# Norm statistics with tokens on the partitions, and two weight jobs run side by side behind six norms

## The reference, cut to what matters

```python
D_MODEL = 1024; SEQ = 512; CTX_LEN = 256; LN_EPS = 1e-5; EPS = 1e-6

def _layer_norm(x, g, b):
    mu = jnp.mean(xf, axis=-1, keepdims=True)
    var = jnp.mean(jnp.square(xf - mu), axis=-1, keepdims=True)
    return (xf - mu) * lax.rsqrt(var + LN_EPS) * g + b

def _rms(x, g):
    return xf * lax.rsqrt(jnp.mean(xf * xf, axis=-1, keepdims=True) + EPS) * g

# layers 0 and 1 (first_block), layer i
u = x * (1.0 + sc1) + sh1
y = mixer(u)                      # 0: mLSTM, 1: differential attention
x = _layer_norm(ALPHA * x + (1.0 + g1) * y, ...)
u = x * (1.0 + sc2) + sh2
y = _conv_ffn(u, ...)             # up-projection 1024 -> 5632, conv, gelu gate, down
x = _layer_norm(ALPHA * x + (1.0 + g2) * y, ...)

# layers 2 and 3 (second_block), for x and, but at the end, for ctx
hx = _rms(x, g) * (1 + cx1) + sx1
x = x + gx1 * mixer(hx)           # 2: conv + Fourier, 3: neighbourhood attention
x = x + gx2 * _mlp(_rms(x, g) * (1 + cx2) + sx2, w1, w2)
```

## Time and profile before

| | |
|---|---|
| median of 3 runs | 3028.05 us (3025.34 to 3028.12) |
| the profiled execution: its time / its span | 3022.47 us / 3020.7 us |
| PE (matmul) busy | 2818.6 us, 93% of the span |
| VectorE, ScalarE, GpSimd busy | 1595.3, 1088.2, 1072.0 us |
| granted TensorE clock, mean | 0.971 of full |
| chain of waits that ended last | PE 84%, VectorE 8%, ScalarE 4% |

### The profile page before, as it was taken

How to read it: one execution, slowest core, us unless ns; L and a number is a source line. 1 busy time by engine, 2 the same in 40 slices (tenths; PEclk the granted TensorE clock), 3 DMA queues, 4 the chain that set the end, 5 groups by cost and what they waited for, 6 DMA issues and landing times.

```text
span 3020.7 us, 38114 instructions
## 1 busy us (share of the span) xinstructions
PE 2818.6 (93%) x13754; PEld 2269.5 (75%) x13754; DVE 1595.3 (53%) x2262; ACT 1088.2 (36%) x1738; POOL 1072.0 (35%) x462
## 2 busy tenths in 40 slices
PE   4998899998998899998899799999997999989998
PEld 3885588886776578886686688888885877768887
DVE  6537796855455797975422422754453376431111
ACT  3333443333465543333411422222224337543222
POOL 2440444444521544444221132323232223334443
PEclk9999999998999899999899899999997999999999
DMA  5350355532421255532111122333331122122222
GB/s 212 113 188 28 118 202 194 191 126 86 142 84 43 98 181 195 188 118 91 44 63 59 39 84 77 127 124 125 123 128 49 63 68 91 54 76 97 98 97 84
DMA packets 89947, 329.70 MB, mean 109 GB/s; under 512 B 9956, under 2 KB 10724, under 8 KB 89320
## 3 DMA queue, kind: packets, MB, share of 16 engines
q1 hardware_dynamic: 85392, 312.21, 30.0%
q10 hardware_dynamic: 4440, 16.00, 1.7%
HBM read 324.50 MB, written 2.10 MB: 108 GB/s over the span
## 4 chain that ended last, share of the span: by engine, by line
PE 84%; DVE 8%; ACT 4%; issue 2%; DMA 1%; POOL 1%; DVEq 0%; ACTq 0%; SPq 0%; POOLq 0%
PE bank L1363 58%; PE junk L1365 9%; PE bank L1104 2%; PE bank L1089 2%; PE bank L1254 1%; PE bank L1380 1%; PE bank L1208 1%; PE junk L1270 1%; PE bank L1287 1%; PE bank L1228 1%; ACT UF L848 1%; PE bank L1130 1%; ACT Uh L848 1%; DVE ADA L1454 1%; DMA ADA<-in_ast 1%
## 5 line engine op out<-in xcount | busy, mean ns | idle before, releaser
L491 POOL TENSOR_TENSOR WL<-RAW,WH 128x1024 fp32r<-128x1024 f32 x392 | 984.1, 2511 | 1740.3 <-ACT WH L792 1249.2
L792 ACT ACTIVATE WH<-RAW 128x1024 fp32r<-128x1024 f32 x292 | 307.0, 1051 | 384.2 <-PE junk L1365 192.0
L1363 PE MATMUL bank<-U1h,WH 128*128 128x512 f32 x960 | 377.7, 393 | 18.7 <-DVE U1l L1736 18.5
L1363 PE MATMUL bank<-U1l,WH 128*128 128x512 f32 x960 | 375.2, 391 | 0.0
L1363 PE MATMUL bank<-U1h,WL 128*128 128x512 f32 x960 | 375.1, 391 | 0.0
L1363 PE MATMUL bank<-Uh,WH 128*128 128x512 f32 x768 | 315.8, 411 | 55.2 <-DVE Ul L1738 54.7
L1363 PE MATMUL bank<-Hh,WH 128*128 128x512 f32 x864 | 342.2, 396 | 11.7 <-DVE Hl L577 11.7
L1363 PE MATMUL bank<-Hl,WH 128*128 128x512 f32 x864 | 339.6, 393 | 0.0
L1363 PE MATMUL bank<-Hh,WL 128*128 128x512 f32 x864 | 338.6, 392 | 0.0
L1363 PE MATMUL bank<-Ul,WH 128*128 128x512 f32 x768 | 307.2, 400 | 0.0
L1363 PE MATMUL bank<-Uh,WL 128*128 128x512 f32 x768 | 306.3, 399 | 0.0
(11 more groups left out here) (348 smaller groups left out, 5002.4 us busy)
## 6 DMA issues: line engine op xcount, KB each, us to landing
RAW<-in_wst SPq DMA_DIRECT2D x392, 512.0 KB, 3.4
ADA<-in_ast SPq DMA_DIRECT2D x192, 512.0 KB, 4.5
NB<-in_nbias ACTq DMA_DIRECT2D x8, 768.0 KB, 4.3
XT<-in_xt SPq DMA_DIRECT2D x1, 2048.0 KB, 15.3
STRIP<-in_strip ACTq DMA_DIRECT2D x8, 256.0 KB, 2.7
CB<-in_cb ACTq DMA_DIRECT2D x4, 512.0 KB, 4.1
DX<-in_dx ACTq DMA_DIRECT2D x1, 2048.0 KB, 7.7
out_xt<-XT SPq DMA_DIRECT2D x1, 2048.0 KB, 6.2
```

Source lines behind the costliest of these rows:

```text
L491: pool.tensor_tensor(WL[:, s4], RAW[:, s2], WH[:, s4].bitcast(F32), ALU.subtract)\
L792: act.activation(WH[:, c % 4], RAW[:, c % 2], ACT.Copy).then_inc(S("hi_done"), 1)
L1363: mm = pe.matmul(bank_of(p, u)[:], w[:, u, k], x[:, k, 0:T], start=st and m == 0, stop=en and m == 2)
```

## The change

Three things.

1. The sums of squares are turned round. `token_sums` uses a block of 128 tokens of the squares as the stationary operand and one column of MEAN as the moving one, so that the result has 128 tokens on the partitions and one column a block: 4 columns for x, 2 more for the context. Root and reciprocal then work on 128x4 or 128x6 elements (SM) in place of 128x512 or 128x768. `widen` brings the result back to one column a token on all partitions: the stationary operand is the scale column read 128 times, the moving one the identity. It lies in PSUM (bank 2 for a LayerNorm, banks 4 and 7 for an RMS norm), where the products now read it. The tile RS is gone. The mean's matmul stays.
2. In a LayerNorm VectorE adds the squares of tiles 5, 6 and 7 onto tile 4 (three instructions behind the centring), so that TensorE sums five tiles and not eight. LayerNorm 3's own sums now come ahead of the context's.
3. Behind six norms (all but LayerNorm 1, whose next phase has its own order) `side_by_side` runs the first two jobs together: for each input tile both jobs' matmuls, once the weights of both are there. Jobs 2 and 3 of the round follow as before. The first round of these phases is peeled out of its loop.

```diff
-                act.activation(RS[:, 0:T], BANK[6][:], ACT.Sqrt, bias=prm("eps5")).then_inc(S("std_done"), 1)
+                act.activation(SM[:, 48:52], BANK[6][:, 0:4], ACT.Sqrt, bias=prm("eps5")).then_inc(S("token_root"), 1)
...
-                steps.link(act.activation(RS[:, 0:T], BANK[5][:], ACT.Sqrt, bias=prm("eps6")))
...
+                n = 6 if ctx else 4
+                act.activation(SM[:, 48:48 + n], BANK[5][:, 0:n], ACT.Sqrt, bias=prm("eps6")).then_inc(S("token_root"), 1)
...
+            def side_by_side(p):
+
+                xh, xl = (U1h, U1l) if p["layer"] < 2 else (Uh, Ul)
+                for u in range(2):
+                    pe.wait_ge(S("lo_done"), p["j0"] + u + 1)
+                pe.wait_ge(S("bank_read"), p["j0"])
+                for k in range(KT):
+                    pe.wait_ge(S("u_ready"), p["fill"] + k + 1)
+                    for u in range(2):
+                        for m, (w, x) in enumerate(((WH, xh), (WH, xl), (WL, xh))):
+                            st, en = k == 0 and m == 0, k == KT - 1 and m == 2
+                            mm = pe.matmul(bank_of(p, u)[:], w[:, u, k], x[:, k, 0:T], start=st, stop=en)
+                            if p["ctx"]:
+                                mm = pe.matmul(BANK[2 + u][:, 0:C], w[:, u, k], x[:, k, T:TC], start=st, stop=en)
+                        if k == KT - 1:
+                            mm.then_inc(S("pe_job"), 1)
...
+            def token_sums(bank, c0, squares, start, stop):
+
+                n = squares.shape[-1] // P
+                for b in range(n):
+                    mm = pe.matmul(bank[:, c0 + b:c0 + b + 1], squares[:, b * P:(b + 1) * P], MEAN[:, 0:1],
+                                   start=start and b == 0, stop=stop and b == n - 1)
+                return mm
+
+            def widen(n, bank, cbank):
+
+                pe.wait_ge(S("token_scale"), n)
+                for b in range(6 if cbank is not None else 4):
+                    dst = (bank if b < 4 else cbank)[:, b % 4 * P:(b % 4 + 1) * P]
+                    ident, scale = bass.broadcast_tensor_aps(IDENT[:], SM[:, 56 + b:57 + b])
+                    mm = pe.matmul(dst, scale, ident, start=True, stop=True)
+                mm.then_inc(S("scale_wide"), 1)
...
                 pe.matmul(BANK[5][:], MEAN[:], ZS[:, 0:T], start=True, stop=True).then_inc(S("mean_sum"), 1)
+                for t in range(5):
+                    if t < 4:
+                        pe.wait_ge(S("squared"), 8 * idx + t + 1)
+                    else:
+                        pe.wait_ge(S("square_rest"), idx + 1)
+                    mm = token_sums(BANK[6], 0, SQ[:, t], t == 0, t == 4)
+                mm.then_inc(S("var_sum"), 1)
                 if idx == 3:
                     for t in range(KT):
                         pe.wait_ge(S("ctx_sq"), t + 1)
-                        pe.matmul(BANK[3][:, 0:C], MEAN[:], UF[:, t, T:TC], start=t == 0, stop=t == KT - 1)
-                for t in range(KT):
-                    pe.wait_ge(S("squared"), 8 * idx + t + 1)
-                    mm = pe.matmul(BANK[6][:], MEAN[:], SQ[:, t], start=t == 0, stop=t == KT - 1)
-                mm.then_inc(S("var_sum"), 1)
+                        token_sums(BANK[5], 4, UF[:, t, T:TC], t == 0, t == KT - 1)
+                widen(idx + 1, BANK[2], None)
...
-                mm = pe.matmul(BANK[5][:], MEAN[:], ZS[:, 0:T], start=True, stop=True)
-                if ctx:
-                    mm = pe.matmul(BANK[6][:, 0:C], MEAN[:], ZS[:, T:TC], start=True, stop=True)
+                mm = token_sums(BANK[5], 0, ZS[:, 0:TC if ctx else T], True, True)
                 mm.then_inc(S("ms_sum"), 1)
+                widen(5 + k, BANK[4], BANK[7] if ctx else None)
...
-                            mm = pe.matmul(BANK[5][:], MEAN[:], UF[:, t, 0:T], start=t == 0, stop=t == KT - 1)
+                            mm = token_sums(BANK[5], 0, UF[:, t, 0:T], t == 0, t == KT - 1)
                         mm.then_inc(S("ms_sum"), 1)
+                        widen(5, BANK[4], BANK[7])
...
-                dve.wait_ge(S("std_done"), idx + 1)
-                link(dve.reciprocal(RS[:, 0:T], RS[:, 0:T]))
+                for t in range(5, KT):
+                    dve.wait_ge(S("squared"), 8 * idx + t + 1)
+                    link(dve.tensor_tensor(SQ[:, 4], SQ[:, 4], SQ[:, t], ALU.add))
+                dve.sem_inc(S("square_rest"), 1)
+                token_scale(idx + 1, 4)
                 for t in range(KT):
-                    dve.tensor_tensor(XT[:, t], XT[:, t], RS[:, 0:T], ALU.mult).then_inc(S("normed"), 1)
+                    dve.tensor_tensor(XT[:, t], XT[:, t], BANK[2][:], ALU.mult).then_inc(S("normed"), 1)
...
+            def token_scale(n, w):
+
+                dve.wait_ge(S("token_root"), n)
+                dve.reciprocal(SM[:, 56:56 + w], SM[:, 48:48 + w]).then_inc(S("token_scale"), 1)
+                dve.wait_ge(S("scale_wide"), n)
```

More of the change, by code:

```diff
@@ L238, in build @@
         TT = at("TT", [2, TC], A_T)
-        RS = at("RS", [TC], A_T)
         UF = at("UF", [KT, TC], A_Y)
@@ L375, in first, with starts_behind_norm @@
             return p["kind"] == kind and p["layer"] == layer and not (p.get("group") or 0)
+        def starts_behind_norm(p):
+            return any(first(p, *what) for what in (("up", 0), ("up", 1), ("ab", 2), ("mlp_up", 2), ("na_q", 3), ("mlp_up", 3)))
         NA_J_END = next((p["j0"] for p in PHASES if first(p, "res2", 3)))
@@ L840, in rms_act @@
                 act.wait_ge(S("ms_sum"), k + 1)
-                steps.link(act.activation(RS[:, 0:T], BANK[5][:], ACT.Sqrt, bias=prm("eps6")))
-                if ctx:
-                    steps.link(act.activation(RS[:, T:TC], BANK[6 if k else 3][:, 0:C], ACT.Sqrt, bias=prm("eps6")))
-                act.sem_inc(S("rms_root"), 1)
+                n = 6 if ctx else 4
+                act.activation(SM[:, 48:48 + n], BANK[5][:, 0:n], ACT.Sqrt, bias=prm("eps6")).then_inc(S("token_root"), 1)
                 for t in range(KT):
@@ L1347, in head_norm_pe @@
                 mm.then_inc(S("n_ms"), 1)
+            def side_by_side(p):
[13 more added lines that the diff above has]
+                            mm.then_inc(S("pe_job"), 1)
             def stream(i, p):
-                for u in range(4):
+                after_norm = is_first(i) and starts_behind_norm(p)
+                if after_norm:
+                    side_by_side(p)
+                for u in range(2 if after_norm else 0, 4):
                     j = i * 4 + (p["j0"] + u)
@@ L1417, in _ @@
                 else:
-                    rounds(pe, p["n"] // 4, lambda i, p=p: stream(i, p), peel=peeled(p) or p["kind"] in ("v", "na_k"))
+                    rounds(pe, p["n"] // 4, lambda i, p=p: stream(i, p), peel=peeled(p) or p["kind"] in ("v", "na_k") or starts_behind_norm(p))
                 if p["kind"] == "v":
@@ L1745, in rms @@
                 w = TC if ctx else T
-                dve.wait_ge(S("rms_root"), k + 1)
-                link(dve.reciprocal(RS[:, 0:w], RS[:, 0:w]))
+                token_scale(5 + k, 6 if ctx else 4)
                 for t in range(KT):
@@ L1754, in rms @@
                                                 XT[:, t].rearrange("p (r w) -> p r w", r=ROWS),
-                                                RS[:, 0:T].rearrange("p (r w) -> p r w", r=ROWS), ALU.mult)
+                                                BANK[4][:].rearrange("p (r w) -> p r w", r=ROWS), ALU.mult)
                     else:
-                        ins = dve.tensor_tensor(UF[:, t, 0:T], XT[:, t], RS[:, 0:T], ALU.mult)
+                        ins = dve.tensor_tensor(UF[:, t, 0:T], XT[:, t], BANK[4][:], ALU.mult)
                     if ctx:
-                        ins = dve.tensor_tensor(UF[:, t, T:TC], CT[:, t], RS[:, T:TC], ALU.mult)
+                        ins = dve.tensor_tensor(UF[:, t, T:TC], CT[:, t], BANK[7][:, 0:C], ALU.mult)
                     ins.then_inc(S("rms_normed"), 1)
```

## The result

The changed kernel takes 2983.2 us (median of 4 runs) against 3026.7 for the kernel before on the same chip: a ratio of 0.986 [0.983, 0.989], 43.5 us less, where 31 were forecast. Measured once more later (after_again), again beside the kernel before, it took 2989.9 against 3016.6: 26.7 us less. The median of all eight runs after is 2988.4, that of all 35 runs before 3025.3: 37 us. The profiled execution after took 2977.8 us, its span 2976.0.

What follows compares the result with a forecast made beforehand. TensorE's work (84% of the chain of waits) plus holes at eight norms bound the kernel. Statistics 7.1 and side-by-side jobs 24.2 make 31.3 us off 3028.05: 2997 us; forecast 2983 to 3011, range with rivals A and B 2963 to 3017.

Steps and rivals of the forecast that it cites:

- Unit price and clock: New sums and widen: a small fp32 load-and-matmul pair costs 0.11 us at full clock, 0.21 us at half.
- Rival A: Faster side, for the new sums: full clock or 0.11 us a pair, 2967 us; chance 0.2.
- rival C: Slower side: load and matmul of a pair don't overlap, 0.54 us a pair at half clock, 3117 us; chance 0.07.
- Root to product: LayerNorms: root, reciprocal, handovers and widen up to the product take 3.0 us.
- The norms: All statistics at LayerNorms 0 to 3 and RMS norms 0 to 3 together gain 7.1 us.
- LayerNorm 3 with RMS norm 0: Context pairs ahead of widen and x's pairs behind it delay the input: a loss of 4.3 us.
- Side by side: First two jobs run together behind six norms: gains of 24.2 us in sum.
- The wait for the bank: Job 2 waits for the first job's bank: 1.05 us behind RMS norm 1, 0.8 behind RMS norm 3.
- Behind LayerNorm 2: PE wins 3.2 us, but VectorE's chain makes its wait grow from 3.97 to about 7: gain 0.2.
- Behind LayerNorm 0: PE wins 3.9 us; at most 1.2 arrives, perhaps 0.7 from a shorter GpSimd pass: gain 1.9.
- My sign of failure for this place: A phase behind LayerNorm 0 ending 4 us sooner after its first input would make the forecast wrong.
- Rival B: Second jobs' gain mostly given back: some 12 us remain beside 3 of the statistics, 3013 us; chance 0.1.

Runs made afterwards that it cites:

- f1: Changed kernel plus spare 512-column matmuls where TensorE would be idle in the norms: 2972.6 us, ratio 0.982.
- i1: Changed kernel, with VectorE adding the context's squares and x's squares 5 to 7 before TensorE sums them in LayerNorm 3 and RMS norm 0: 2975.6 us, ratio 0.983.
- w1: Kernel before, with one of VectorE's two products with each ADA tile left out behind LayerNorm 2: 3013.4 us.
- w2: Changed kernel, with one of VectorE's two products with each ADA tile left out behind LayerNorm 2: 2984.8 us (two runs).
- g1: Changed kernel, but ScalarE copies each LayerNorm's widened scale from PSUM to SBUF, where VectorE's product reads it: 2995.3 us, ratio 0.990.
- e1: Kernel before plus the side-by-side jobs alone, with the old statistics: 2995.5 us, ratio 0.990.
- c1: Changed kernel with the edits of i1 and f1 together: 2965.5 us (5 runs), ratio 0.981.
- c2: c1 plus spare matmuls at the first matmuls of the down phases of layers 0 and 1: 2959.1 us (5 runs), ratio 0.981.
- e2: Kernel before plus the new statistics alone, all jobs one after the other: 3004.9 us, ratio 0.994.
- g2: g1 plus spare matmuls where TensorE waits for the last two low parts at the down phases of layers 0 and 1: 2990.9 us (four runs).

## Why the prediction was right, and where not

The forecast of 2997 lies 14 us above the first median and 7 above the second, inside the range. Its 31 us stand against 29 to 35 in the traces at equal pace. The mechanisms named are there, but for one stretch, where the size was near by luck (below).

- **Unit price and clock.** 0.21 us at half clock; 8.69 / 40 = 0.217 in every LayerNorm (also 8.70 and 13.82 / 64 = 0.216). That the sums would run at half clock was my estimate: no run had shown it for one-column pairs; the earlier trace rows has PE busy at a low clock with other matmuls (0.52 and 0.58). The traces show 0.50 from 346.50 to 355.00 after and, in f1, under 13.81 us of pairs without a break. At the head of RMS norm 1, still at full clock in part (0.82 from 1694.5 to 1696.5), 12 pairs took 1.80, as forecast; in after_again the clock was already at 0.50 there and they took 2.72. Rival A (2967) asked for a full clock in the sums or 0.11 us a pair, rival C for 0.54 a pair; neither is there.
- **Root to product, about 3 us**: 2.6.
- **The norms brought 10.85 for 7.1**, and 8.05 in after_again. In the first trace every one is 0.2 to 0.8 better than its term; 1 us at a single norm is within what two executions differ by. In LayerNorm 0, sums and chain together took 345.16 to 356.53, 11.37, where I had 11.7, and I had then taken 0.8 for a working that gave 1.0: both halves of the 0.5 that is missing there.
- **LayerNorm 3 with RMS norm 0**: lost 3.6 for 4.3, by the mechanism named; i1 takes it away at its price.
- **Side by side.** Behind the RMS norms (0 to 3) 6.38, 5.7 to 6.0, 6.59, 2.11 for 6.85, 6.0, 7.25, 2.0; in after_again 6.55 and 1.51 for the last two. The 5 us at half clock behind RMS norm 1 were my estimate too; the jobs ran at 0.50 from 1704.85 to 1709.3 after, 4.5 us, and from 1712.52 to 1717.8 in after_again. The wait for the bank, forecast at 1.05 us behind RMS norm 1 and 0.8 behind RMS norm 3, is there:

```profile
1725.18 0.47 PE L1384 MATMUL bank<-Uh,WH 128*128 128x512 f32 x1 [1.09 <-issue]
...
2630.61 0.47 PE L1384 MATMUL bank<-Uh,WH 128*128 128x512 f32 x1 [0.86 <-issue]
```

- **Behind LayerNorm 2** PE's wait grew from 3.97 to 6.23 (7 forecast). w1 and w2 show that TensorE brings 3.7 to it without the second pass (3.2 forecast), and 1.2 with it. They also show that VectorE's work isn't the only thing that eats the gain: at the end of the stretch nothing of it is left in w2.
- **Behind LayerNorm 0** the size was nearly right and the reason wrong. The forecast let at most 1.2 of the 3.9 arrive, and put perhaps 0.7 down to a shorter GpSimd pass; the pass was 1.5 us shorter, by the product's input in PSUM, which I hadn't seen in the diff and on which 3.1 us of the stretch hang (g1). And the 1.2 had no clock in it: without the PSUM input the side-by-side jobs bring 0.2 to 0.5 here (e1, g1), since TensorE then waits twice in a row and the clock is low for 3.4 us (0.51 in e1, 0.52 in g1). My sign of failure for this place, a phase that ends 4 us sooner, did come (3.57). That 3.57 and 1.9 are within 2 us of each other is luck.
- **Rival B** (much given back) happens behind LayerNorm 2, and behind LayerNorm 0 where the product reads SBUF (e1, g1).
- **What no step had**: that two executions of one kernel differ by 10 us in a stretch without waits. It made the gain in the first pair of traces look 10 us larger than its mechanisms.

## What to carry to other kernels

A sum over partitions with one moving column cost by the pair here, not by the column (0.217 us with one column, 0.24 to 0.26 with 128), and left TensorE at a clock of 0.50 (f1, 13.81 us of pairs): add tiles on an idle engine first, and put spare wide matmuls where it would stand idle, at the next seam too, or that seam takes the gain back (f1 and c1 against c2). When an engine that is ahead is made faster still, price not only the wait it then meets but what the clock does behind it. And before a gain is put down to an edit, compare a stretch that the edit doesn't touch, and a second execution of the same kernel.

## What the runs showed of the hardware

Pairs of short waits of PE, some 2.2 us from one to the next, stand at several seams, the second always about 1.2 us. Where the first was 0.94, 1.14, 1.36, 2.79 or 3.15 us (e1, g1, w2, c1, f1), the clock fell each time, to 0.50 to 0.52 for 3.4 us or more. Where it was 0.68, it fell in two of 26 places (layer 0 of e2 and c1), and where it was 0.5, in three of 13 (layer 1 of after_again, g2 and c2). At a single wait of 0.93 (after) or 1.21 (after_again) in layer 0 it stayed at 1.00. So the same waits can cost the clock or not; the longer ones did every time here. What decides in the short ones is open. The loss of 3.68 us in g1 is 1.21 of wait, 1.7 of low clock, and 0.8 that I can't place.

The pace of the layer-2 MLP is 8.48 or 8.32 us a job and stays for the whole stretch; both occurred on each of three chips, and with one and the same kernel (after, after_again). The stretch before it has the same two paces, not always the same one as the MLP, and in i1 and c2 the pace changes on the way. The granted clock is 1.00 at both (from 1850 to 2200 in before and after). What sets the pace is open; no run here was made to tell it.
